# Layer ends by token halves, norm factors on the products, and a warm start in a two-block fp32 transformer kernel

## What is computed

```python
def hybrid_layer(x, ...):             # first block, twice
    h = x @ w_in                      # 2048 -> 6672: attention, gated linear attention, memory attention
    y = concat([y_a * silu(a_z), y_b * silu(b_z), y_m * silu(m_z)])
    return layer_norm(ALPHA * x + y @ w_out, ln_g, ln_b)

def second_block(x, ...):             # once
    h = rms_norm(x, norm_mix_pre)
    proj = h @ w_in                   # 2048 -> 11272
    y_a = hgrn2_mixer(a_q, a_f, a_i, a_g, ...) @ w_up_a    # gated linear attention, 8 heads
    y_b = fox_mixer(b_q, b_k, b_v, b_f + b_fox_f) @ w_up_b # attention with forget gates
    merged = sigmoid(g_a) * y_a + sigmoid(g_b) * y_b
    x = x + rms_norm(merged @ w_o, norm_mix_post)
    gate, up = split(rms_norm(x, norm_ffn_pre) @ w_ffn_in) # 2 x 5632
    return x + rms_norm((silu(gate) * up) @ w_ffn_down, norm_ffn_post)
```

## Time and profile before

| | |
|---|---|
| median of 3 runs | 2449.51 us (2446.97 to 2449.54) |
| the profiled execution | 2452.5 us, its span 2450.7 us |
| PE busy | 2407.2 us, 98% of the span |
| DVE, ACT busy | 1499.5 us (61%), 1267.3 us (52%) |
| DMA | 458.84 MB, mean 187 GB/s |
| chain that ended last | 92% PE, 3% DVE, 3% ACT, 1% DMA |

### The profile page before, as it was taken

The page is one execution under the profiler, slowest core; times in us unless marked ns, Lnnn a source line. Parts: engine busy times, 40 slices in busy tenths (PEclk is TensorE's granted clock), DMA queues, the critical chain, the costliest instruction groups (busy, mean ns, idle before and its releaser), DMA issues.

```text
span 2450.7 us, 32972 instructions
## 1 busy us (share of the span) xinstructions
PE 2407.2 (98%) x13098; PEld 2076.5 (85%) x13098; DVE 1499.5 (61%) x1693; ACT 1267.3 (52%) x1710; POOL 7.5 (0%) x14
## 2 busy tenths in 40 slices
PE   8999999999999998999999999998999999999998
PEld 7888888888888877888898888887888888888887
DVE  6575566766755667575765566755655555555454
ACT  5444465444455644555664457444554555554443
POOL 0000000000000000000000000000000000000000
PEclk9999999999999998999999999998999999999999
DMA  8544557665545664554545545575556565557554
GB/s 297 196 152 151 178 171 258 217 218 172 163 147 172 235 204 147 181 164 155 164 155 183 177 156 181 185 244 179 197 174 195 183 195 192 182 187 256 191 196 138
DMA packets 127834, 458.84 MB, mean 187 GB/s; under 512 B 13600, under 2 KB 20288, under 8 KB 124736
## 3 DMA queue, kind: packets, MB, share of 16 engines
q1 hardware_dynamic: 126720, 450.38, 55.9%
q0 software_dynamic: 816, 6.29, 0.7%
q10 hardware_dynamic: 144, 0.07, 0.0%
HBM read 448.30 MB, written 8.39 MB: 186 GB/s over the span
## 4 chain that ended last, share of the span: by engine, by line
PE 92%; DVE 3%; ACT 3%; DMA 1%; issue 1%; DVEq 0%; SPq 0%; ACTq 0%
PE banks L83 91%; ACT wh L47 1%; DMA raw<-in_w_in_f 1%; PE banks L86 1%; DVE wl L50 1%; ACT tb L47 0%; DVE z_buf L59 0%; ACT sm_s L47 0%; DVE le L50 0%; DVE f_buf L59 0%; DMA raw<-in_kv_t 0%; DVE lqe L50 0%; DVE x_buf L59 0%; ACT t L47 0%; DVE o_buf L50 0%
## 5 line engine op out<-in xcount | busy, mean ns | idle before, releaser
L50 DVE TENSOR_TENSOR wl<-raw,wh 128x1024 fp32r<-128x1024 f32 x808 | 974.8, 1222 | 412.1 <-ACT wh L47 406.3
L47 ACT ACTIVATE wh<-raw 128x1024 fp32r<-128x1024 f32 (+1 forms) x811 | 835.6, 1051 | 386.2 <-PE banks L83 275.8
L83 PE MATMUL banks<-xx,wh 128*128 128x512 f32 (+1 forms) x3888 | 983.7, 395 | 2.3 <-ACT xx L47 2.3
L83 PEld LDWEIGHTS banks<-xx,wh 128*128 128x128 f32 (+1 forms) x3888 | 699.4, 189 | 135.4 <-ACT xx L47 3.0
L83 PEld LDWEIGHTS banks<-xx,wl 128*128 128x128 f32 x3840 | 525.1, 191 | 38.1
L83 PE MATMUL banks<-xx,wl 128*128 128x256 f32 x3840 | 536.3, 283 | 0.0
L83 PE MATMUL banks<-wh,xx 128*128 128x512 f32 x1536 | 383.5, 390 | 0.0
L83 PEld LDWEIGHTS banks<-wh,xx 128*128 128x128 f32 x1536 | 286.9, 188 | 59.0
L83 PE MATMUL banks<-wl,xx 128*128 128x512 f32 x768 | 207.9, 389 | 0.0
L83 PEld LDWEIGHTS banks<-wl,xx 128*128 128x128 f32 x768 | 144.2, 188 | 30.0
L83 PE MATMUL banks<-wh,yy 128*128 128x512 f32 x512 | 127.7, 390 | 3.7 <-ACT wh L47 3.7
(11 more groups left out here) (203 smaller groups left out, 1570.4 us busy)
## 6 DMA issues: line engine op xcount, KB each, us to landing
raw<-in_w_in_f SPq DMA_DIRECT2D x304, 512.0 KB, 3.7
raw<-in_w_ffn_f SPq DMA_DIRECT2D x176, 512.0 KB, 4.4
raw<-in_w_ffn_down SPq DMA_DIRECT2D x88, 512.0 KB, 3.5
raw<-in_w_in_t SPq DMA_DIRECT2D x80, 512.0 KB, 3.6
raw<-in_w_out_t SPq DMA_DIRECT2D x64, 512.0 KB, 4.7
raw<-in_w_o_t SPq DMA_DIRECT2D x32, 512.0 KB, 4.4
raw<-in_kv_t SPq DMA_DIRECT2D x16, 512.0 KB, 5.3
raw<-in_kv_f SPq DMA_DIRECT2D x16, 512.0 KB, 4.4
```

The source lines that it names most:

```text
L47: return lambda e: e.activation(*a, **k)
L50: return lambda e: e.tensor_tensor(*a, **k)
L83: return lambda e: e.matmul(*a, **k)
```

## The change

- **Start.** Eleven matmuls whose result nobody reads are put first on PE's queue. The first memory tile arrives as two half pieces, and the constants are loaded behind unit 16.
- **Places.** Weight places become a list from which `split` takes the first and to which `run_unit` gives back. Ahead of each boundary four more places are added from free SBUF (offsets 8, 16, 24, 40 KB and 48, 56, 64, 80 KB), and the look-ahead grows from 2 to 6 over four units; in the next group it falls back to 2 and the four are dropped.
- **First boundary.** The second token half of w_out's last group runs with the transposes of the first half in it. z is only standardized (one tensor_scalar per 128x1024); gain x column weight and bias x column weight (gw3, bw3) are applied to the transposed tiles, in 128x128 pieces on ACT or DVE. The next group is the token-major one (v, plan_t(t2[0]) comes first): four half units for the first token half, then the transposes and features of the second half with three splits between, four half units for it, then four whole units. ln_g, ln_b, the sums of squares and the store come after (`finish_sum`, a post).
- **Second boundary.** The same with x1; the first gate group and the first up group of the FFN become token-major, and their product (tokens on partitions) is transposed into first_h. Groups 1 to 10 are as before.
- **Factors.** The token factor of rms_norm is no longer in X. Each feature-major product of block 2 is multiplied by a row (row3), each token-major one by a column while ACT copies it; in the FFN z gets row4 and z*sigmoid(z) gets it once more, which stands for the up product.

The core of the diff:

```diff
+        asleep = at("asleep", 100, P, f32r)
+        keep_awake(11, asleep[:, :], 7, (op("dve", lambda e: e.memset(asleep[:, :].bitcast(f32), 0.0)),))
...
+        def more_places(offsets, fence):
+            for k in offsets:
+                h, l = at(f"xh{len(extra)}_{k}", k, 1024, f32r), at(f"xl{len(extra)}_{k}", k + 4, 1024, f32r)
+                extra.append((h, l))
+                places.insert(0, (extra[-1], fence, fence))
+            state["ramp"] = len(offsets)
...
+        def cols_t_halves(made, turn_on):
+            pr = pair()
+            ns = [take(0) for _ in range(4)]
+            free = [bank_free[pr[t]] for t in range(2)]
+            half_pass(X, pr, 0, ns, 0, True, False, True, [made[0, u // 2] + (free[0] if u == 0 else ()) for u in range(4)])
+            state["ahead"], state["leave"] = AHEAD, True
+            turn_on()
+            half_pass(X, pr, 1, ns, 0, True, False, False, [made[1, u // 2] + (free[1] if u == 0 else ()) for u in range(4)])
+            for u in range(4, 8):
+                n = take()
...
+                tok = run_unit(n, his, los, made[0, u // 2] + made[1, u // 2])
+                step_all()
...
         def join(pr, tok, dst, scale=None, waits=(), row=None):
...
+            if row is not None:
+                r2 = row[0].rearrange("p (o s) -> p o s", o=1).to_broadcast([P, 2, S])
+                d = op("dve", lambda e: e.tensor_tensor(d2, d2, r2, ALU.mult), d, row[1])
...
+        def feature(t, q, b):
+            f, tok = f_buf[:, (q % 2) * 512:(q % 2) * 512 + 512], turned[t, q]
+            for j in range(4):
+                k, o, i = 4 * q + j, f[:, j * P:(j + 1) * P], banks[b][:, j * P:(j + 1) * P]
+                if q % 2:
+                    a = op("dve", lambda e: e.tensor_scalar(o, i, gw3[:, k:k + 1], bw3[:, k:k + 1], ALU.mult, ALU.add), ...)
+                else:
+                    a = op("act", lambda e: e.activation(o, i, ACT.Identity, scale=gw3[:, k:k + 1], bias=bw3[:, k:k + 1]), ...)
...
+            c = op("act", lambda e: e.activation(h, f3, ACT.Copy), a)
+            d = op("dve", lambda e: e.tensor_tensor(l, f3, h.bitcast(f32), ALU.subtract), c, a)
...
+        tok0 = half_pass(Y, pr, 0, tok, 0, False, True, True)
+        ag, r = standardize(0, add(0, tok0))
+        z0 = [scaled(0, c, (ag, r)) for c in range(2)]
+        def turn_first():
+            for q in range(2):
+                turned[0, q] = turn_half(z_buf, 0, q, 4 + q, (z0[0],))
+        tok1 = half_pass(Y, pr, 1, tok, 0, False, True, False, hook=turn_first)   # hook ahead of its 4th unit
+        for q in range(2, 4):
+            turned[0, q] = turn_half(z_buf, 0, q, 4 + q, (z0[1],))
+        feature(0, 0, 4)
+        feature(0, 1, 5)
+        ag, r = standardize(1, add(1, tok1))
+        feature(0, 2, 6)
+        feature(0, 3, 7)
+        z1 = [scaled(1, c, (ag, r)) for c in range(2)]
+        def second_half():
+            for q in range(4):
+                turned[1, q] = turn_half(z_buf, 1, q, 4 + q, (z1[q // 2],))
+                feature(1, q, 4 + q)
+                if q:
+                    split(len(cut))
...
+        def feature4(t, q, b, free):          # second boundary: 4 x ACT (scale column), 4 x DVE, 128x128 from PSUM
+            for j in range(4):
+                a = op("act", lambda e: e.activation(X.hi_of(k, t * P, P), i, ACT.Identity, scale=NFP(k)), turned[t, q], *free)
+            for j in range(4):
+                d = op("dve", lambda e: e.scalar_tensor_tensor(out=X.lo_of(k, t * P, P), in0=i, scalar=NFP(k), ...), ...)
...
+        tok0 = half_pass(X, pr, 0, tok, 8, False, True, True)
+        r = last_block(0, tok0)
+        z0 = [post_sum(0, c, (r, rx) + toks[0]) for c in range(2)]
+        sq0 = [post_squares(0, c, z0[c]) for c in range(2)]
+        tok1 = half_pass(X, pr, 1, tok, 8, False, True, False, hook=turn_first4)
+        for q in range(2, 4):
+            turned[0, q] = turn_half(x_buf2, 0, q, 4 + q, (z0[1],))
+        feature4(0, 0, 4, (tok0,))
+        feature4(0, 1, 5, (tok0,))
+        r = last_block(1, tok1)
+        feature4(0, 2, 6, (tok0,))
+        feature4(0, 3, 7, (tok0,))
+        z1 = [post_sum(1, c, (r, rx) + toks[1]) for c in range(2)]
...
+            d = op("dve", lambda e: e.tensor_tensor(u, z, u, ALU.mult), got[0])
+            r2 = row4.rearrange("p (o s) -> p o s", o=1).to_broadcast([P, 2, S])
+            mids.append(op("dve", lambda e: e.tensor_tensor(tiled(u), tiled(u), r2, ALU.mult), d, rows4[1]))
```

More of the change, by code:

```diff
@@ L269, in plan_narrow, with give_back @@
             plan(w, hi="narrow")
-        sent, cut = [], []
-        used = {}
+        sent, cut, t_const = [], [], []
+        place = {}
+        places = [((wh[n], wl[n]), (), ()) for n in range(NH)]
+        extra = []
+        def more_places(offsets, fence):
[4 more added lines that the diff above has]
+            state["ramp"] = len(offsets)
+        def give_back(n, hi_tok, lo_tok):
+            if not (state["leave"] and any(place[n] is x for x in extra)):
+                places.append((place[n], (hi_tok, cut[n][1]), (lo_tok,)))
         def send(n):
@@ L291, in split @@
             if hi is not None and not narrow:
-                r, hi_free, lo_free = tiled(r), tuple(free), tuple(free)
+                r, hi_free, lo_free = tiled(r[:, 0:S * src.shape[1]]), tuple(free), tuple(free)
             else:
[L294 to L298, removed]
+                place[n], hi_free, lo_free = places.pop(0)
+                hi, lo = place[n][0][:, :], place[n][1][:, :]
             first = hi
@@ L355, in drain, with take @@
                 step_lanes()
-        def take(ahead=AHEAD):
+        def take(ahead=None):
             n = state["next"]
             state["next"] += 1
-            while len(cut) < min(n + ahead + 1, len(units)):
+            if state["ramp"]:
+                state["ramp"] -= 1
+                state["ahead"] += 1
+            while len(cut) < min(n + (state["ahead"] if ahead is None else ahead) + 1, len(units)):
                 split(len(cut))
             return n
[L365 to L370, removed]
         bank_free = {n: () for n in range(8)}
@@ L489, in cols_t @@
                 return pr, tok
-            ns = [take(0) for _ in range(4)]
[L491 to L496, removed]
-                                           False, u == 3 and kk == 1)
+            return pr, [take(), take(), take(0), take(0)]
@@ L1378, in half @@
             def half(i, pr, tok):
-                d = join(pr, tok, gates[n][:, i * 512:(i + 1) * 512], waits=free(i))
+                d = join(pr, tok, gates[n][:, i * 512:(i + 1) * 512], waits=free(i), row=rows[0])
                 posts.append((None, gate_post(i, d, n)))
@@ L1400, in build @@
             toks = list(c_ready)
[L1401 to L1402 removed]
+            cols_f(X, joined(toks, q_, scale=SC, waits=free, row=rows[0]))
+            cols_f(X, joined(toks, k_, waits=free, row=rows[0]))
             pr, tok = cols_t(X)
[L1404 removed]
+            ready = tuple(toks) + tuple(value(v_[:, t * 512:t * 512 + 512], pr[t], tok, factor3[t], free) for t in range(2))
             def add_decay(o, h, t, nk, g=g):
```

493 lines of the change are left out of this document (269 added, 224 removed).

## The result

The changed kernel is slower: 2476.57 us as a median of 4 runs (2475.01 to 2478.08) against 2448.24 (2446.88 to 2449.54) for the kernel before in the same session. The ratio is 1.0116, with a 95% interval of 1.0098 to 1.0133. The forecast was 2432.7, range 2424 to 2442, 93% for faster. It was wrong in sign and by 44 us. The step that failed is the mixer behind the first boundary: the prediction let the change cost 1.5 us there, and it cost 35; the deferred part of the first boundary, priced at nothing, cost another 10.

The account below looks back on a forecast made before the run. TensorE was taken as the bound, busy 2407 of 2450.7 us. Start -2.9, first boundary -5.6, second boundary -9.8 and products +1.5 summed to -16.8, giving a median of 2432.7 us, range 2424 to 2442.

Parts of the forecast that it names:

- Part 4: Factors on products in block 2 and FFN: 76 added DVE products, mostly hidden by DVE idle time, costing +1.5 us.
- the deferred sum: After the first boundary: deferred gain, bias, squares and factor run beside whole units, costed at nothing.
- Start, -2.9: Kernel start: unread matmuls bring unit 0 to full speed, gain 2.3; a smaller first memory piece gains 0.6 us.
- Rival C2: Start: unit 0 stays slow because the eleven matmuls end too early; 2.3 us back, 2435; chance 0.1.
- First boundary, -5.6: Layer 1 to block 2: token halves overlap the norm with PE work, gaining 5.6 us although the clock falls again.
- The walk up to 973.5: First boundary: PE idles 5.4 us before the second half's transposes; token-major group ends at 973.5, shifted by the first stretch.
- Second boundary, -9.8: Mixer to FFN: token halves shorten the wait and the clock stays up, gaining 9.8 us.
- No idle piece is over 2.2 us here: Second boundary: the reason given for the clock staying up, with 10.2 us gained before smaller terms.
- Products, +1.5: Block 2 and FFN: factor products delay PE slightly in linear attention, costing 1.5 us.
- part 5: Weight places and queues: extra splits, loads and the later store of x cost nothing.
- Rival D: Linear attention and gate stages: DVE becomes the bound at about 95% of a stretch; 2459 to 2485 us; chance 0.04.
- three signs of being wrong: PE waiting on wh or wl in gate stages, a second-boundary clock dip, or the first idle piece gone.

Follow-up runs that it names:

- e2: Kernel before with one line added, setting the posts' pace to two after block 2's first group; one execution, 2468.48 us.
- e4: Kernel before with the new start alone (eleven unread matmuls, half memory piece, constants behind unit 16); 2448.11 us, ratio 0.9994.
- e1: Changed kernel with the posts' pace set back to one in any case in block 2's first forget half; 2446.95 us, ratio 0.999.
- e13: e1 with the deferred sum reordered, each square a step behind its bias pass, and one more step before the spread matmuls; 2439.79 us, ratio 0.996.
- e8: Changed kernel with the old first boundary and no factor products in block 2, keeping new start and second boundary; 2435.01 us, ratio 0.9943.
- e7: e1 with the 76 factor products left out, so the output lacks that factor; 2443.26 us, ratio 0.9976.
- e6: e1 with the deferred sum two steps at a time, later spread, and 18 unread matmuls before the second half's transposes; 2447.58 us, ratio 0.9995.
- e10: e8 with 34 unread matmuls in the wait at the old first boundary; 2436.68 us, ratio 0.9947.

## Why the prediction was wrong

Two steps failed. Part 4 let the added work cost +1.5 in the mixer, reckoned from DVE's share of busy time; the stretch N to R grew by 35.4, by the order of the queues under a pace of two. And the same part put the deferred sum at nothing; T0 to N grew by 4.7 where it was to shrink by 5.6. The second boundary came as forecast. By terms:

*Start, -2.9.* The stretch to T0 is 5.7 shorter in the kernel after and 2.2 to 6.2 shorter in the profiled executions of the other kernels with the new start (and 1.5 shorter in e2, which has the old one), but e4's ratio, which rests on ten runs, gives 1.5, and its interval goes from a gain of 3.9 to a loss of 0.7. Rival C2 happened in three of thirteen starts, the kernel after among them: unit 0's eight high matmuls took 2.59, 2.90 and 3.78 there, and 2.11 to 2.27 in the others. The Trainium skill, TensorE: Matmul & The Clock Gate, Part 1, says that the warming moment differs from run to run; the rows agree. The weights' arrival varies too (waits of 0 to 2.1). Only 2.6 of the 5.7 are the start (the ninth unit at 28.88, for 31.45 in the earlier trace rows). Most of the rest is three waits on wh near 860 in before, 2.7 together, that the profiled execution of after does not have; e1's list of waits has 4.2 on wh in 5 again.

*First boundary, -5.6.* The walk up to 973.5 was right within 0.2 at the places named above, with 0.77 for the tensor_scalar (0.80 taken), 1.50 for four ACT operations of 128x128 (1.6) and 1.36 for four on DVE (1.15). The step that failed is a sentence of part 4: "The deferred gain, bias, squares and factor ... run beside whole units ... I cost them at nothing". I had not walked that part. It cost the whole gain: T0 to N +4.7 for -5.6, 10.3 off. e13 shows that some 6 of these are the order in which the sum was queued; the last wait of 3.9 is still there in e13, and what would be left without it was not tried.

*Second boundary, -9.8.* Right: -10.2 in the kernel after, -10.1 in e8, without a fall of the clock, with the 40 products of the FFN in the number. The reason given for the clock, "No idle piece is over 2.2 us here", is not one that holds elsewhere: in the mixer the clock fell after waits of 1.26. That it stayed up here may be luck; why it did is open.

*Products, +1.5.* With the queues in the old order the amount was about right: the products of block 2 in that stretch cost 1.1 (e1 less e7, 3.4 by the ratios) and the stretch 3.4 in all. The mechanism was not, and in the kernel after it decides. The step "one join per four units (11.2 us) adds 6 points there" priced DVE's share, where the wait of PE hangs on the place of lqe in the queue. I had seen that the steps go two per unit and not asked until when; part 5, "Places, queues", puts the queues at nothing and does not name the posts. That is worth 20.9 in the kernel before (e2), 32.0 with the products (after less e1).

*Rival D* had the right sign and a time near the truth (2459 to 2485) for a wrong reason: DVE at 95%. It is at 63% in N to R (441.8 of 696.1), as in before, and no slice of the page has it at 80%. The free points that spoke against D are 16 by its own numbers (79 to 95), not 18. The nearness of the time is luck.

*Signs named.* A dip at the first boundary and none at the second, DVE at 63% (62%): right. Unit 0's matmuls in about 2.0: 2.59. "lqe waits of 3 to 4 us in sum": wrong, 20.5, and 3.1 once the pace is right (e1). None of the three signs of being wrong appeared: all three watch the boundaries and the gate stages, and the loss was in the mixer.

## What to carry to other kernels

Where engines work fixed queues, the price of an added pass is not its share of the engine but what stands behind it: the same products cost 1 to 3 us or 16.7. Walk deferred work to its end like the rest, and set each square or copy that waits for the other engine behind the weight splits, not ahead of them. When a change touches a pacing flag, look for where it is set back, and on which path it isn't. The boundary by token halves paid where little is deferred (the second), and at the first no gain is shown even with its sum in the better order. Holding the clock gave nothing in the two waits where it was tried, where DVE and ACT ended the stretch.

## Not expected of the hardware

The length of a wait does not tell whether the clock falls behind it. Seven of the twelve waits on lqe in the kernel after are of 1.26, each with sixteen small matmuls behind it. Two of them, with the unit behind each:

```profile
1141.94 1.97 PE L83 MATMUL banks<-lqe 128*128 128x64 f32 x16 [1.26 <-DVE lqe L50]
1143.72 3.59 PE L83 MATMUL banks<-xx,wh 128*128 128x512 f32 x8
...
1233.09 1.97 PE L83 MATMUL banks<-lqe 128*128 128x64 f32 x16 [1.26 <-DVE lqe L50]
1234.87 2.09 PE L83 MATMUL banks<-xx,wh 128*128 128x512 f32 x8
```

Four of the seven were followed by a fall and three were not; a wait of 1.98 was not either. In e2 a wait of 0.96 was followed by eight high matmuls in 3.55, and one of 2.10 by eight in 2.09. Behind the wait of 1.93 shown under "The mixer" the granted clock was 0.76 in 1057 to 1060 and 0.50 in 1060 to 1063. At the second boundary idle pieces of 1.1, 1.0 and 0.9 left the clock up. What decides was not tried. In the kernel after the lower clock took 15.5 of the 35.4 us of N to R, nearly as much as the waits themselves (19.9). And an idle piece filled with unread matmuls, with the clock at 1.00 through it, gave nothing twice (e6, e10).
